# Setup and input projection of a hybrid decoder block as one program, tiles 0 and 1 by token chunk

## The reference

```python
shift, scale, gate = jnp.split(silu(c) @ w_ada + b_ada, 3, axis=-1)
h = rms_norm(x, norm_w) * (1.0 + scale) + shift
a_val, a_glu, a_gate, cq, ckv, k_pe, b_gate, g_a, g_b = split(h @ w_in)   # 6720 columns
q_in, kv_in = rms_norm(cq, q_norm_w), rms_norm(ckv, kv_norm_w)            # 256 columns each
k_rope = apply_rope(k_pe, cos, sin)                                       # 64 columns
u = causal_depthwise_conv(a_val * sigmoid(a_glu), conv_w, conv_b)         # 31 taps, 1024 channels
...  # layer norm, two output products, 8 heads of attention, the gated residual, a final RMSNorm
```

## Time and profile before

| | us |
|---|---|
| Median of 3 runs | 2746.11 (2741.65 to 2747.65) |
| The profiled execution, its own time | 2742.87 |
| Its span | 2741.1 |
| TensorE busy | 2592.6 (95%) |
| VectorE busy | 1757.6 (64%) |
| ScalarE busy | 853.9 (31%) |
| GpSimd busy | 642.4 (23%) |
| Granted TensorE clock, mean | 0.981 |

### The profile page before, as it was taken

One profiled execution on the slowest core, in us unless ns is written; L12 is line 12 of the kernel. 1 busy time (PEld: TensorE's weight loads), 2 busy tenths in 40 slices (PEclk: granted clock), 3 DMA queues, 4 the chain that ended last, 5 costly groups with the idle time before them and its releaser, 6 DMA issues. The chain is left out here.

```text
span 2741.1 us, 32651 instructions
## 1 busy us (share of the span) xinstructions
PE 2592.6 (95%) x12185; PEld 2132.1 (78%) x12185; DVE 1757.6 (64%) x2107; ACT 853.9 (31%) x1686; POOL 642.4 (23%) x593
## 2 busy tenths in 40 slices
PE   3699999999999999999699999999999989999998
PEld 3477888888888888878578878878878768888887
DVE  5765769789798797756267677677677622132442
ACT  3432111111111111143155555555555530201221
POOL 1232211111111111133032332332332320322422
PEclk9799999999999999999899999999999999999999
DMA  7143212121221121277932122122121065666542
GB/s 263 42 151 106 64 54 77 46 77 51 67 84 46 54 83 41 69 238 268 289 103 100 44 82 105 42 78 105 47 73 69 24 222 170 192 218 210 186 157 77
DMA packets 203184, 306.74 MB, mean 112 GB/s; under 512 B 18281, under 2 KB 126893, under 8 KB 193100
## 3 DMA queue, kind: packets, MB, share of 16 engines
q1 hardware_dynamic: 196812, 284.37, 31.5%
q0 software_dynamic: 6272, 20.98, 2.5%
HBM read 202.01 MB, written 103.28 MB: 111 GB/s over the span
## 5 line engine op out<-in xcount | busy, mean ns | idle before, releaser
L52 PE MATMUL ps_proj<-h_hi,w_hi 128*128 128x512 f32 x1696 | 666.6, 393 | 13.6 <-POOL w_lo L650 11.4
L53 PE MATMUL ps_proj<-h_lo,w_hi 128*128 128x512 f32 x1696 | 661.9, 390 | 0.0
L54 PE MATMUL ps_proj<-h_hi,w_lo 128*128 128x512 f32 x1696 | 661.6, 390 | 0.0
L810 DVE SCALAR_TENSOR_TENSOR acc<-u,taps_t,acc 128x2048 f32<-128x2048 f32 x240 | 629.0, 2621 | 8.5
L52 PEld LDWEIGHTS ps_proj<-h_hi,w_hi 128*128 128x128 f32 x1696 | 319.6, 188 | 82.7 <-POOL w_lo L650 11.6
L53 PEld LDWEIGHTS ps_proj<-h_lo,w_hi 128*128 128x128 f32 x1696 | 319.8, 189 | 68.2 <-issue 2.2
L54 PEld LDWEIGHTS ps_proj<-h_hi,w_lo 128*128 128x128 f32 x1696 | 319.6, 188 | 66.7
L650 POOL TENSOR_TENSOR w_lo<-raw,w_hi 128x1024 fp32r<-128x1024 f32 x53 | 167.8, 3166 | 812.1 <-ACT w_hi L545 812.1
L1627 POOL TENSOR_SCALAR prob<-prob,rinv 128x512 f32<-128x512 f32 (+2 forms) x320 | 197.0, 636 | 355.3 <-DVE rinv L1581 355.2
L1586 DVE TENSOR_TENSOR pt_lo<-ps_t,pt_hi 128x512 fp32r<-128x512 f32 (+1 forms) x320 | 194.4, 609 | 97.9 <-ACT pt_hi L1509 93.7
L1509 ACT ACTIVATE pt_hi<-ps_t 128x512 fp32r<-128x512 f32 (+1 forms) x320 | 169.7, 532 | 239.6 <-PE ps_t L1421 239.6
(11 more groups left out here) (199 smaller groups left out, 4056.6 us busy)
## 6 DMA issues: line engine op xcount, KB each, us to landing
qlat<-qlat_dram SPq DMA_DIRECT2D x32, 1024.0 KB, 5.6
raw<-in_w_in_dram SPq DMA_DIRECT2D x52, 512.0 KB, 6.4
wada<-in_w_ada_dram SPq DMA_DIRECT2D x8, 1024.0 KB, 12.7
ga_dram<-lat SPq DMA_DIRECT2D x8, 1024.0 KB, 5.0
gb_dram<-lat SPq DMA_DIRECT2D x8, 1024.0 KB, 5.0
agate_dram<-lat SPq DMA_DIRECT2D x8, 1024.0 KB, 5.0
conv_dram<-acc SPq DMA_DIRECT2D x8, 1024.0 KB, 3.9
bgate_dram<-lat SPq DMA_DIRECT2D x8, 1024.0 KB, 5.0
```

What stands on the lines that cost most here:

```text
L52: pe.matmul(out, wh, xh, start=first, stop=False)
L53: pe.matmul(out, wh, xl, start=False, stop=False)
L54: return pe.matmul(out, wl, xh, start=False, stop=last)
L810: dve.scalar_tensor_tensor(acc[:], u[:, n:n + S], tap(n), acc[:], ALU.mult, ALU.add).then_inc(conv_tap if n < TAPS - 1 else conv_done, 1)
```

## The change

The two programs become one, `front_phase`, so one program end and one barrier less stand between them.

- **Order of loading.** First c, then x of group 0, two blocks of `w_ada` (now four of 512 columns, each in two halves), the parameter rows and taps, the weights of tiles 0 and 1, the other two blocks, and the rest of x. All have places of their own: `w_ada` lies in chunks 1 and 2 of the room of h_hi and h_lo, x in chunk 3 of it and in `u`, `acc`, `sg`, `part`. SP waits for nothing there.
- **c first.** silu(c) is made from a transpose of its own (C_COL), ahead of the other parameters.
- **Tiles 0 and 1 by chunk.** For each of the 32 pieces of h TensorE does that piece's six matmuls for tiles 0 and 1 and then the transposes of the piece four further on; the first four pieces' transposes stand before, and those of pieces 8 to 11 all behind piece 7. The weights of tiles 0 and 1 are split before.
- **Squares of x** go one by one behind ACT's pieces 0 to 11.
- **Tile 2's weights** have a slot of their own (`w2_hi` over `full`, `w2_lo` over the raw weights).
- **Angles** are made after h. The positions are loaded into `ang` itself.
- **Gate** pieces are all eight in tile 4 (KEY), two after each chunk, and read out by pairs.
- **Latents.** The means use other banks (MEAN_BANK) and other times: (tile, chunk) to means is MEANS. The second latent is normalised beside tiles 5 and 6, and its chunks are taken out without waiting for `part`.
- **Key.** DVE rotates it straight out of the banks of tile 4 in two halves of 1024 tokens, ACT and DVE split it whole, and tile 6 waits for the banks by `kpe_read`.

The diff, cut to its core:

```diff
-def setup_phase(k):
...
-        nc.all_engine_barrier()
-def projection_phase(k):
+def front_phase(k):
...
+    AHEAD = 4
+    N_PIECE = NC_ * KT
+    X_BANKS = [[1, 5, 2, 6], [3, 7, 2, 6], [0, 4, 3, 7], [1, 5, 0, 4]]
+    MEAN_BANK = [4, 5, 6, 7, 6, 7, 2, 3]
...
+        wada_at = [[half[:, kh * KH:(kh + 1) * KH, chunk(c)] for kh in range(2)] for c in (1, 2) for half in k.under_h]
...
+                row(*rows[0], c_in)
+                load_x(0)
+                ada(0)
+                ada(1)
+                for r in rows[1:]:
+                    row(*r, params_in)
+                sp.dma_start(taps, k.conv_w.rearrange("o t c -> (o t) c")).then_inc(params_in, 16)
+                tile_weights(0)
+                tile_weights(1)
+                ada(2)
+                ada(3)
+                for g in range(1, NC_):
+                    load_x(g)
...
+                for tile in (2, 3):
+                    sp.wait_ge(lo_made, tile - 1)
+                    tile_weights(tile)
+                sp.wait_ge(x_turned, KT)
+                sp.dma_start(ang.bitcast(I32), k.positions.to_broadcast([P, S])).then_inc(pos_in, 16)
...
+                store_part(0)
+                store_part(1)
+                sp.wait_ge(chunk_mm, 3 * NC_)
+                tile_weights(KEY)
+                sp.dma_start(wada[0][:], w_ada[:, :, 2 * D:2 * D + GCOLS]).then_inc(gate_first_in, 16)
...
             @block.scalar
+                for i in range(QB):
+                    square_x(i)
+                split_hi(0)
+                split_hi(1)
+                act.wait_ge(ada_vec, 4)
+                for n in range(N_PIECE):
+                    turn_out(n)
+                    if n < TT - QB:
+                        square_x(QB + n)
+                    c, t = divmod(n - KT, KT)
+                    if c >= 0 and t == AHEAD - 1:
+                        evict(0, c)
+                        evict(1, c)
+                        if c < 2:
+                            square(c)
+                split_hi(2)
+                evict(0, NC_ - 1)
+                evict(1, NC_ - 1)
+                split_hi(3)
+                root(0)
+                root(1)
...
+                for c in range(NC_):
+                    if 1 <= c < NC_ - 1:
+                        root(c + 1)
+                    hi_of(c)
+                    act.wait_ge(part_lo_done, c + 1)
+                    evict(2, c)
+                split_hi(KEY)
...
             @block.gpsimd
+                scale_x(0)
+                split_lo(0)
+                split_lo(1)
+                for g in range(1, NC_):
+                    scale_x(g)
+                split_lo(2)
+                split_lo(3)
+                lo_of(0)
+                gate_piece(1)
+                for c in range(1, NC_):
+                    lo_of(c)
+                split_lo(KEY)
+                gate_piece(2)
+                gate_piece(3)
+                split_lo(5)
+                for n in range(4, N_GATE):
+                    gate_piece(n)
...
             @block.tensor
+                for n in range(N_PIECE):
+                    g, t = divmod(n, KT)
+                    pe.wait_ge(h_lo_done, n + 1)
+                    for tile in range(2):
+                        wh, wl = weights(tile)
+                        mm = split3(pe, ps[:, bank(tile, g), :], wh[:, t, :], wl[:, t, :], k.h_hi[:, t, chunk(g)],
+                                    k.h_lo[:, t, chunk(g)], t == 0, t == KT - 1)
+                        if t == KT - 1:
+                            mm.then_inc(chunk_mm, 1)
+                    held = n < KT and n >= KT - AHEAD
+                    if n == KT - 1:
+                        for m in range(KT, KT + AHEAD):
+                            turn_x(m)
+                    elif not held and n + AHEAD < N_PIECE:
+                        turn_x(n + AHEAD)
...
+                MEANS = {(2, 0): (0, 1), (3, 0): (2,), (3, 1): (3,), (5, 0): (4, 5), (6, 0): (6,), (6, 1): (7,)}
...
+                        if tile == KEY:
+                            for n in (2 * c, 2 * c + 1):
+                                pe.wait_ge(gate_step, KT * (n + 1))
+                                pe.wait_ge(chunk_out, out_no(3, c))
+                                pe.matmul(ps[:, NC_ + c, n % 2 * GCOLS:(n % 2 + 1) * GCOLS], k.mean_mat[:], gate_acc[n % 2],
+                                          start=True, stop=True).then_inc(gate_mm, 1)
```

More of the change, by code:

```diff
@@ L465, in last_store, with raw_need, weights, bank @@
             return 16 * (1 + stores_before(PRE + TILES.index((kind, H - 1)) + 1))
+        def raw_need(tile):
+            return 16 * sum(3 if t == KEY else 1 for t in range(tile % 2, tile + 1, 2))
+        def weights(tile):
+            if tile == 2:
+                return k.w2_hi, k.w2_lo
+            return w_hi[tile % 2], w_lo[tile % 2]
+        def bank(tile, c):
+            return tile % 2 * NC_ + c
         with nc.Block() as block:
@@ new lines, in turn_out, with evict @@
+                def turn_out(n):
+                    g, t = divmod(n, KT)
+                    act.wait_ge(x_turned, n + 1)
+                    if n >= 2:
+                        act.wait_ge(h_lo_done, n - 1)
+                    act.activation(full[n % 2], ps[:, X_BANKS[g][t % 4], :], ACT.Identity, scale=gain[:, t:t + 1],
+                                   bias=shift[:, t:t + 1]).then_inc(full_done, 1)
+                def evict(tile, c):
+                    act.wait_ge(chunk_mm, mm_no(tile, c))
+                    act.activation(lat[:, tile % LT, chunk(c)], ps[:, bank(tile, c), :], ACT.Copy).then_inc(chunk_out, 1)
@@ L603, in ln_means @@
+                split_hi(KEY)
+                for c in range(NC_):
+                    evict(3, c)
+                    if c < 2:
+                        square(NC_ + c)
+                split_hi(5)
+                split_hi(6)
+                root(NC_)
+                root(NC_ + 1)
                 def ln_means():
@@ L690, in load_z @@
                     pool.dma_start(z_gate[s], k.agate_dram[z_rows(h), z_cols(h)]).then_inc(z_in[s], 16)
-                for tile in range(PRE, N_TILES):
+                for tile in range(PRE + 1, N_TILES):
                     if tile == TAIL + 2:
@@ new lines, in _ @@
+                pe.wait_ge(consts, 6)
+                pe.wait_ge(c_in, 16)
+                pe.transpose(ps_par[:, C_COL:C_COL + KT], prm[R_C:R_C + KT, :],
+                             k.ident[0:KT, 0:KT]).then_inc(c_turned, 1)
+                ada_products(0)
+                for n in range(AHEAD):
+                    turn_x(n)
+                ada_products(1)
+                pe.wait_ge(params_in, 16 * len(rows))
+                pe.transpose(ps_par[:, 0:R_END], prm[:], k.ident[0:R_END, 0:R_END]).then_inc(params_t, 1)
@@ L936, in _ @@
[L936 to L942 removed]
+        nc.clear_and_free_semaphores(sems)
+        nc.all_engine_barrier()
```

827 lines of the change are left out of this document (394 added, 433 removed).

## The result

The changed kernel took 2707.85 us (median of 4 runs, 2706.28 to 2709.62), the kernel before 2746.88 (2741.65 to 2748.53, 4 runs): ratio 0.9861, interval 0.9844 to 0.9878. Forecast: 2707, range 2694 to 2728, faster. The profiled execution took 2709.62 (span 2707.7) against 2742.87 (2741.1).

The account below looks back on a forecast made before the run. TensorE paces everything after tile 6's end, so the change only shifts that point: -43 us up to tiles 0 and 1's end, +7 behind, sum -36, from 2742.9 to 2707 us; range 2694 to 2728.

Parts of the forecast that it names:

- that one point: End of tile 6, at 291.5 us in the old kernel; the unchanged stretch behind it runs at TensorE's pace.
- forecast -43: Up to the end of tiles 0 and 1: done at about 117 against 160.4 us, so 43 us earlier.
- +7: From tiles 0 and 1 to tile 6's end: moved work and stalls make 131.1 us into 138.3.
- The start, -3.5 forecast: Up to the first piece of h: at about 47 us instead of 50.77, 3 to 4 us earlier.
- 47.80 to 50.77, 3.0, less 1: From the last modulation step to ACT's first piece: the old 3.0 us, less 1 for transposes no longer in that path.
- 64 + 1.5 + 2: Loop over 32 pieces of h: 64 us at TensorE's pace, 1.5 for held transposes, 2 for low clock at entry.
- go into ACT's slack: In the loop, the evictions of tiles 0 and 1 cost nothing, since transposes run four pieces ahead.
- and if not, 2 us: End of the loop: splitting tile 2's weights is hidden behind TensorE's last pieces, otherwise costing 2 us.
- Low clock (0.07): Rival: the loop's clock stays near 0.50, a piece takes 3.4 us, +43, so 2750 us, slower; chance 0.07.
- Hand-over pace of 2.6 (0.16): Rival: hand-over between ACT, DVE and POOL paces the loop's pieces at 2.6 us, +16, 2725 us; chance 0.16.
- Costlier gates (0.13): Rival: latents and gates cost more, tile 4 slower and stalls doubled, +15, 2722 us; chance 0.13.
- Stalls mostly hidden: Rival: the added stalls in tiles 2 to 5 are mostly hidden, -15, 2692 us; chance 0.08.

Follow-up runs that it names:

- x_late: The changed kernel with only the interleaving undone: all 32 pieces of h first, then tiles 0 and 1 by chunk; 2727.41 us, ratio 0.9945.
- x_fill2: The changed kernel with idle matmuls (25, 9, 9) on TensorE while it waits for the modulation's sums at the start; 2706.42 us, ratio 0.9865.
- x_spread: The changed kernel with ScalarE's evictions and squares of a finished chunk spread over the following pieces of h; 2705.63 us, ratio 0.9857.
- x_hold: The changed kernel with the held transposes of token group 1 let go in two steps instead of all behind one piece; 2707.62 us, ratio 0.9867.
- x_noang: The changed kernel with DVE's nine angle steps cut to 8 of 2048 columns, so its angles are wrong; 2700.66 us, ratio 0.9847.
- x_gate: The changed kernel with gate sums set between tile 4's matmuls and sums of squares 4 and 5 moved earlier, their means later; 2708.13 us, ratio 0.9872.
- x_order: The changed kernel with the weights of tiles 0 and 1 loaded behind the second half of the modulation's weights; 2708.93 us, ratio 0.9876.
- a_again: The changed kernel run once more, unchanged, for the spread; 2710.98 us, ratio 0.9878.

## Why the prediction was right, and where it was not

**The point that moves, and what doesn't.** "Whatever the change does is the shift of that one point": shown for the head stages, 1010.11 against 1010.40. The shift came out at -38.9 (254.62 and 254.19 in the repeats, so -37) for a forecast -36, the time at -39.0, -31.9 and -36.2 against the kernel before in the three sessions. At the first mean it was -42.8 for a forecast -43, and behind it +4.0 (+5.6 and +6.8 in the repeats) for +7. Direction, path and the two large terms were right. That 2707.85 lies 0.85 from 2707 is luck: the errors below, of 1 to 7 us each, mostly cancel, and 5.5 us behind tile 6, forecast at nothing, happen to fill the rest.

**What the overlap was worth.** The prediction's -43 was "3.5 from the start, 4.5 from the removed barrier, split and tail, the rest two tiles put under the making of h". That rest, 35, is too much for the overlap: x_late, which has none, is already 18.5 us earlier at the first mean, and only 1.5 + 4.4 of that are the first two terms. The other 12.5 are a shorter making of h (8.5) and shorter tiles 0 and 1 (4.0). The overlap gave 24.4. The sum held all the same, since it was built from when the pieces start and how long one takes, and not from this division.

**The start, -3.5 forecast, -1.2 measured.** Eight products took 4.9, forecast 5.1, and block 3 never waited, so it had landed by 40.3 (38 forecast, 32 to 42). But block 2 had landed only at 34.91, and DVE's two blocks behind it end at 45.2, forecast 43.1: the loads were the bound one block earlier than I thought. The step that failed is "47.80 to 50.77, 3.0, less 1": it took 4.4. The 3.0 was read behind a block of 256 columns, whose sums are eight one-column matmuls; the new block has 512 columns and sixteen of them, 3.58 us for 1.86, both at the slow pace (1.95 for sixteen with the clock held up, x_fill2). The kernel before:

```profile
47.85 1.86 PE L306 MATMUL ps_ada<-mean_mat,ada_acc 128*128 128x1 f32 x8 [1.04 <-DVE ada_acc L266]
```

And the transposes held that first piece up by 0.4 us (`gain` was made at 50.40), not by 1. The 2 us of margin took up nearly half of the 4.5.

**The loop, 64 + 1.5 + 2 forecast from 49.5, done at 117; measured about 116.3 from 51.71.** So 64.6 instead of 67.5. Two terms were off and partly cancel: a piece cost 1.83 and not 2.09 (transposes 0.12 each, not 0.18), -7 over 28 pieces; and ScalarE's pile at the first eviction, which I had put at nothing ("go into ACT's slack"), cost 2.3 and the clock behind it, 3.5 in all in this trace by x_spread. The wait at the held block was 1.6 as forecast (1.5), though x_hold gives only a part of it to that block. The pile is the term I would mend: a cover holds piece by piece, not on average. The split of tile 2's weights, forecast hidden ("and if not, 2 us"), held the first mean up by 1.1.

**Behind the loop, +7 forecast, +4.0 measured** (135.1 us for 131.2). With the 1.1 above, the stalls were 11.3, 13.3 and 12.7 in the three traces and not 17.9. The places were right: angles late into the third sum (2.0 at 143.3, forecast 2.4), the next sum (0.6, and 2.2 in both repeats, forecast 3.1), tile 4's weights (0.2, forecast 1.3), tile 4 (3.1 of gate waits, forecast 7.6), tile 5 behind the gate read-out (2.8, forecast 1.5), tile 6 (1.4, forecast 2). What I overpriced most is tile 4: two pieces took 7.9 us and not 9. The means were underpriced: from the one at 152.14 to the first matmul it is 0.56, and that matmul takes 0.63 to the next where 0.23 is usual, so 0.96 for a single mean and 7.5 for all eight (two pairs, four single) instead of 5.6. The clock was granted at 0.94 from 143 to 198 and at 0.81 in the 6.9 us behind: 55 x 0.06 + 6.9 x 0.19 = 4.6 lost, forecast 4. With 108.8 for the chunks and 2 for the gate sums these terms give 133 of the 135.1; the last 2 us I can't place.

**The rivals.** Low clock (0.07): TensorE's granted clock was 0.93 over the loop, 0.50 only up to 55 us. By the rule of the Trainium skill cited in the prediction ("TensorE: Matmul & The Clock Gate", "A second HAM failure mode: psum-queue depth-cycling"), told there of a bf16 kernel, a loop that cycles through banks with small gaps should swing; the trace disagrees, with 1.00 from 90 to 115 while matmuls and transposes alternate between banks, and pieces 1.83 apart. In the loop it fell only behind the wait of 2.3 us, in five of the eight traces with this loop, and x_spread took that fall away with the wait. Hand-over pace of 2.6 (0.16): no, 1.83. Costlier gates (0.13): no. Stalls mostly hidden (0.08): a part of it, 4.6 to 6.6 of the 15.

**What stays open.** From tile 6's end to the end of the span the changed kernel took 2455.0, 2454.0 and 2455.1 us in three traces, the kernel before 2449.5 and 2449.9. No code there was changed. The difference is spread over projections (+1), the value phase and its entry, attention (834.3 to 835.1 against 832.6 and 833.2) and output (+1). The other kernels with the merged program show everything between, 2449.3 (x_noang) to 2455.7 (x_gate), with attention at 831.4 to 836.0. The overlap alone doesn't set it: x_noang and x_order (2450.9) have it and lie low, x_late has none and lies at 2451.8. Traces of one kernel agree within 1.1 us, so chance alone is unlikely too, but with one trace for most kernels that isn't shown. What in the front moves the later stages by up to 6 us no run here isolates, and it is why -38.9 at tile 6 is -33 in the same trace's span.

## What to carry to other kernels

Find the one stretch that runs at the engine's pace and does not change, and price an edit by the shift of its start. When an edit does several things at once, undo the main one alone: here half of the gain at tile 6 didn't need it. A wait read off the old kernel has to be scaled to the new shapes (eight sums became sixteen). When work is put under other work, check each engine's cover at every step of the loop: here every average had slack, and the losses were one pile of ScalarE operations and one block of held transposes, each a short wait, now and then with a low clock behind it. Small losses that a measurement can't tell singly can be removed together and then measured.

## What was not expected of the hardware

Sixteen one-column float32 matmuls take 3.58 us at half clock and 1.95 at full, so idle matmuls ahead of them pay only if they end in time. Six products of DVE on 128x512 took 4.06 us alone and 8.23 while POOL split weights for most of that time (40.70 to 46.39), twice the time.

And a row of the granted clock can disagree with the matmuls: the windows of a_again say 1.00 for 50 to 55 us, while the timeline of the same trace has the matmuls 0.43 apart, the pace of half clock.

```profile
50.00:55.00 5.00, 3.80 (x11) 1.00 1.07 380
```

```profile
52.19 0.63 PE L54 MATMUL ps_proj<-h_hi,w_lo 128*128 128x512 f32 x1
52.62 0.63 PE L52 MATMUL ps_proj<-h_hi,w_hi 128*128 128x512 f32 x1
```

The kernel before has the same disagreement: its row says 1.00 from 47.85 to 49.70 us, where eight one-column matmuls take 1.86 us, the pace that sixteen in 3.58 have at a row of 0.50. Where the two differ I went by the spacing.
